# Decoded sequences' scores and values: heads modulo four in the four 32-row strips of PSUM

## The reference, cut to what matters

```python
c_all = cumsum(concat([lf_past, logf]))                    # log forget gates, per head
s_past = einsum('bqhd,bkhd->bhqk', q, k_past) * ATTN_SCALE + c_new[..., None] - c_past[:, :, None, :]
s_new = where(tri, einsum('bqhd,bkhd->bhqk', q, k) * ATTN_SCALE + c_new - c_new', -inf)
p = softmax(concat([s_past, s_new], axis=-1))
return einsum('bhqk,bkhd->bqhd', p[..., :P], v_past) + einsum('bhqk,bkhd->bqhd', p[..., P:], v)
```

## Time and profile before

| what | us |
|---|---|
| median of 3 runs | 2475.67 |
| lowest, highest | 2474.58, 2480.06 |
| the profiled execution's own time | 2478.78 |
| its span, first to last instruction | 2477.0 |
| head loop, first `page_scores` to the first L1617 | 1058.66 to 1126.62 |
| logits and softmax of the decoded sequences | 1126.62 to 1138.37 |
| values, first L1648 to the copy L1204 | 1138.37 to 1172.68 |
| `in_m` starts | 1184.66 |

### The profile page before, as it was taken

How to read it: one execution, slowest core, us unless ns; L and a number is a source line. 1 busy time by engine, 2 the same in 40 slices (tenths; PEclk the granted TensorE clock), 3 DMA queues, 4 the chain that set the end, 5 groups by cost and what they waited for, 6 DMA issues and landing times.

```text
span 2477.0 us, 47822 instructions
## 1 busy us (share of the span) xinstructions
PE 2400.4 (97%) x17547; PEld 2329.1 (94%) x17547; DVE 1248.7 (50%) x1850; ACT 843.6 (34%) x1109; POOL 83.7 (3%) x96
## 2 busy tenths in 40 slices
PE   7999999999999999898899897999999999999998
PEld 6999999999999999687899775999999999999998
DVE  6554444444554554552457675465444444455443
ACT  4333333333333443320234323343333333333322
POOL 2000000000000000000000241000000000000000
PEclk9999999999999999898999887999999999999999
DMA  6555555555544455433355341455555445555553
GB/s 165 170 166 169 163 163 170 171 165 169 165 163 164 151 165 165 137 123 134 122 162 162 117 118 38 163 160 166 166 169 161 162 170 170 169 162 160 170 161 131
DMA packets 175655, 383.82 MB, mean 155 GB/s; under 512 B 18949, under 2 KB 44669, under 8 KB 175245
## 3 DMA queue, kind: packets, MB, share of 16 engines
q1 hardware_dynamic: 172736, 375.98, 47.9%
q0 software_dynamic: 2432, 5.57, 0.7%
q10 hardware_dynamic: 416, 1.32, 0.2%
HBM read 373.09 MB, written 9.70 MB: 155 GB/s over the span
## 4 chain that ended last, share of the span: by engine, by line
PE 93%; DVE 4%; ACT 1%; issue 1%; DMA 0%; POOL 0%; ACTq 0%; DVEq 0%; POOLq 0%
PE ps L1415 28%; PE ps L1417 28%; PE ps L1416 28%; PE ps L1597 1%; PE ps L1654 1%; DVE w_lo L846 1%; PE ps L1760 1%; PE ps L1584 1%; PE ps L1461 1%; PE ps L1751 1%; PE ps L1498 1%; PE ps L1468 1%; PE ps L1532 0%; PE ps L1555 0%; DVE xt L872 0%
## 5 line engine op out<-in xcount | busy, mean ns | idle before, releaser
L846 DVE TENSOR_TENSOR w_lo<-w_raw,w_hi 128x1024 fp32r<-128x1024 f32 (+1 forms) x690 | 788.9, 1185 | 1038.3 <-ACT w_hi L560 1037.7
L560 ACT CAST w_hi<-w_raw 128x1024 fp32r<-128x1024 f32 (+1 forms) x690 | 669.3, 1018 | 1304.2 <-PE ps L1417 1301.2
L1415 PE MATMUL ps<-x_hi,w_hi 128*128 128x288 f32 (+1 forms) x2752 | 815.8, 296 | 5.2 <-DVE w_lo L846 3.2
L1417 PE MATMUL ps<-x_hi,w_lo 128*128 128x288 f32 (+1 forms) x2752 | 813.3, 296 | 0.0
L1416 PE MATMUL ps<-x_lo,w_hi 128*128 128x288 f32 (+1 forms) x2752 | 807.9, 294 | 0.0
L1415 PEld LDWEIGHTS ps<-x_hi,w_hi 128*128 128x128 f32 x2752 | 517.0, 188 | 6.4 <-DVE w_lo L846 3.3
L1416 PEld LDWEIGHTS ps<-x_lo,w_hi 128*128 128x128 f32 x2752 | 521.4, 189 | 0.1
L1417 PEld LDWEIGHTS ps<-x_hi,w_lo 128*128 128x128 f32 x2752 | 517.8, 188 | 0.0
L1415 PE MATMUL ps<-hid_hi,w_hi 128*128 (+1 forms) x1376 | 407.2, 296 | 1.5 <-DVE X L1017 1.5
L1416 PE MATMUL ps<-hid_lo,w_hi 128*128 (+1 forms) x1376 | 406.9, 296 | 0.0
L1417 PE MATMUL ps<-hid_hi,w_lo 128*128 (+1 forms) x1376 | 406.8, 296 | 0.0
(11 more groups left out here) (408 smaller groups left out, 1573.2 us busy)
## 6 DMA issues: line engine op xcount, KB each, us to landing
w_raw<-in_w_down SPq DMA_DIRECT2D x178, 512.0 KB
w_raw<-in_w_gate SPq DMA_DIRECT2D x320, 256.0 KB
w_raw<-in_w_up SPq DMA_DIRECT2D x320, 256.0 KB
w_raw<-in_w_in SPq DMA_DIRECT2D x64, 512.0 KB
w_raw<-in_w_in SPq DMA_DIRECT2D x64, 384.0 KB
w_raw<-in_w_out SPq DMA_DIRECT2D x32, 512.0 KB
page<-in_cache_k SPq DMA_DIRECT2D x16, 512.0 KB, 3.5
w_raw<-in_w_gate SPq DMA_DIRECT2D x32, 192.0 KB
```

The source lines that it names most:

```text
L560: nc.scalar.copy(w_hi[:, slot, 0:width], w_raw[:, slot, 0:width]).then_inc(w_hi_ready, 1)
L846: nc.vector.tensor_tensor(w_lo[:, slot, 0:width], w_raw[:, slot, 0:width], w_hi[:, slot, 0:width].bitcast(F32), ALU.subtract).then_inc(w_l ...
L1415: mm(out, hi, x_hi[:, k, :], start=first and pair == 0 and s == slots[0], stop=False)
L1417: ins = mm(out, lo, x_hi[:, k, :], start=False, stop=last and pair == 1 and s == slots[-1])
```

## The change

Heads are put in strips by h % 4, and the rows are ordered (h, b, q) in place of (b, h, q).

- `page_scores`: head h of a page writes strip h % 4 of bank 6; heads h and h + 4 share a strip and lie 256 columns apart, and the page half c takes 128 columns. `qz` for sequence b now has, per head, all 32 (b, q) query columns with all but sequence b's zeroed; sequences add up in place.
- New tokens: the products swap their operands (queries stationary, keys moving) and write in four strips of bank 5, at once where the logits are built. The copy `STn`, its semaphore and the two products L1633 go.
- `nl_new`, `nl_past`, `spread`, `PTn` follow the new order; `spread` shrinks to 32x128, the copy to `PTn` becomes plain.
- Values: head h writes strip h % 4 of bank 2 (columns by h // 4), for new tokens and pages. The result is 128x256, so that one copy and two transposes of 128x128 stand in place of two copies and eight transposes.

The diff:

```diff
--- before.py
+++ after.py
@@ -128,7 +128,7 @@
     mask_t = t_("mask_t", [P, 3 * P])
     mask4_q = t_("mask4_q", [SM, SM])
     mask4_t = t_("mask4_t", [SM, SM])
-    spread = t_("spread", [SM, NB * SM])
+    spread = t_("spread", [SM, P])
     sel = t_("sel", [H, H, P], F32R)
     one_hot = t_("one_hot", [P, H, H])
     vecs = t_("vecs", [P, 146])
@@ -217,7 +217,7 @@
             qz = nl_past
 
 
-            pz, out_rows = kpT[:, 0, :].rearrange("p (r n) -> p r n", r=4), kpT[0:SM, 1, :]
+            pz, out_rows = kpT[:, 0, :].rearrange("p (r n) -> p r n", r=4), kpT[:, 1, 0:2 * HD]
 
             flat = [x[:, :, :].rearrange("p h t -> p (h t)") for x in (qa, ka)]
             v_page = ([kn[:, i, :] for i in range(3)] + [page[:, (NB * NPG + i) % 3, :] for i in range(3)]
@@ -225,8 +225,7 @@
             VRING = len(v_page)
 
 
-            PTs, STn = l_("PTs", [P, 512]), l_("STn", [SM, 256])
-            PTn = STn
+            PTs, PTn = l_("PTs", [P, 512]), l_("PTn", [SM, 256])
             Ps = l_("Ps", [P, 2, T])
 
         scope, l_ = area("left")
@@ -749,8 +748,7 @@
                                      accum_out=den[:, k, g2:g2 + 1]).then_inc(sem("sample_exp"), 1)
         act.wait_ge(sem("sample_pT"), 1)
         nc.scalar.copy(PTs[:, :], ps[:, 0, :]).then_inc(sem("sample_pT_ready"), 1)
-        nc.scalar.copy(PTn[:, :].rearrange("p (h b q) -> p b h q", h=H, b=NB),
-                       ps[0:SM, 1, 0:256].rearrange("p (b h q) -> p b h q", b=NB, h=H)).then_inc(sem("sample_pT_ready"), 1)
+        nc.scalar.copy(PTn[:, :], ps[0:SM, 1, 0:256]).then_inc(sem("sample_pT_ready"), 1)
 
 
 
@@ -1031,9 +1029,8 @@
         nc.vector.tensor_scalar(neg_upper4[:, :], upper4[:, :], -1.0, None, ALU.mult)
         nc.vector.tensor_scalar(mask4_q[:, :], lower4[:, :], -1.0, BIG, ALU.add, ALU.mult)
         nc.vector.tensor_scalar(mask4_t[:, :], upper4[:, :], -1.0, BIG, ALU.add, ALU.mult)
-        nc.vector.tensor_copy(spread[:, :].rearrange("p (b h q) -> p b h q", b=NB, h=H),
-                              ident[0:SM, 0:SM].rearrange("p (b q) -> p b q", q=TS).unsqueeze(2)
-                              .to_broadcast([SM, NB, H, TS]))
+        nc.vector.tensor_copy(spread[:, :].rearrange("p (j s) -> p j s", j=4),
+                              ident[0:SM, 0:SM].unsqueeze(1).to_broadcast([SM, 4, SM]))
         nc.vector.memset(one_hot[:, :, :], 0.0).then_inc(sem("one_hot_zero"), 1)
         dve.wait_ge(sem("one_hot_zero"), 1)
         for h in range(H):
@@ -1146,9 +1143,9 @@
             if b >= 2:
                 dve.wait_ge(sem("sT_done"), NPG * (b - 1))
             nc.vector.tensor_tensor(
-                qz[:, b % 2, :].rearrange("p (h g q) -> p h g q", h=H, g=H),
-                qa[:, :, TP + b * TS:TP + (b + 1) * TS].unsqueeze(1).to_broadcast([P, H, H, TS]),
-                one_hot[:, :, :].unsqueeze(3).to_broadcast([P, H, H, TS]), ALU.mult).then_inc(sem("qz_ready"), 1)
+                qz[:, b % 2, :].rearrange("p (h g q) -> p h g q", h=H, g=NB),
+                qa[:, :, TP:T].rearrange("p h (g q) -> p h g q", g=NB),
+                one_hot[:, b, :].unsqueeze(1).unsqueeze(3).to_broadcast([P, H, NB, TS]), ALU.mult).then_inc(sem("qz_ready"), 1)
 
         dve.wait_ge(sem("qk_normed"), 2 * H)
         queries_apart(0)
@@ -1165,18 +1162,16 @@
                 o_copy(h - 1)
         o_copy(H - 1)
 
-        nc.vector.tensor_scalar(nl_new[:, :].rearrange("p (b h q) -> p b h q", b=NB, h=H),
-                                LF[0:SM, 2, 0:H].unsqueeze(1).unsqueeze(3).to_broadcast([SM, NB, H, TS]), -1.0, None, ALU.mult)
+        nc.vector.tensor_scalar(nl_new[:, :].rearrange("p (h s) -> p h s", h=H),
+                                LF[0:SM, 2, 0:H].unsqueeze(2).to_broadcast([SM, H, SM]), -1.0, None, ALU.mult)
         dve.wait_ge(sem("lf_past_loaded"), 16 * NB * NPG)
         dve.wait_ge(sem("sT_done"), NB * NPG)
         for c in range(NPG):
             last = nc.vector.tensor_scalar(
-                nl_past[:, c, :].rearrange("p (b h q) -> p b h q", b=NB, h=H),
-                lf_past[:, :, :].rearrange("p (b c) h -> p b c h", c=NPG)[:, :, c, :].unsqueeze(3)
-                .to_broadcast([P, NB, H, TS]), -1.0, None, ALU.mult)
+                nl_past[:, c, :].rearrange("p (h b q) -> p h b q", b=NB, h=H),
+                lf_past[:, :, :].rearrange("p (b c) h -> p h b c", c=NPG)[:, :, :, c].unsqueeze(3)
+                .to_broadcast([P, H, NB, TS]), -1.0, None, ALU.mult)
         last.then_inc(sem("nl_ready"), 1)
-        dve.wait_ge(sem("sT_done"), NB * NPG + 1)
-        nc.vector.tensor_copy(STn[:, :], ps[0:SM, 7, 0:256]).then_inc(sem("sT_ready"), 1)
         dve.wait_ge(sem("sample_logits"), 1)
         nc.vector.tensor_reduce(mx[:, 0, :], ps[:, 6, :].rearrange("p (g s) -> p g s", g=2), AX.X, ALU.max)
         link(nc.vector.tensor_reduce(mx[:, 1, :], ps[:, 5, 0:2 * SM].rearrange("p (g s) -> p g s", g=2), AX.X, ALU.max))
@@ -1196,12 +1191,10 @@
                 dve.wait_ge(sem("sample_pv"), p - 3)
             nc.vector.tensor_tensor(
                 pz[:, p % 4, :].rearrange("p (h b q) -> p h b q", h=H, b=NB),
-                PTs[:, c * 256 + b * SM:c * 256 + (b + 1) * SM].rearrange("p (h q) -> p h q", h=H).unsqueeze(2)
-                .to_broadcast([P, H, NB, TS]),
+                PTs[:, c * 256:(c + 1) * 256].rearrange("p (h b q) -> p h b q", h=H, b=NB),
                 one_hot[:, b, :].unsqueeze(1).unsqueeze(3).to_broadcast([P, H, NB, TS]), ALU.mult).then_inc(sem("pz_ready"), 1)
         dve.wait_ge(sem("sample_pv"), NB * NPG)
-        for half in range(2):
-            nc.vector.tensor_copy(out_rows[:, half * 512:(half + 1) * 512], ps[0:SM, 2 + half, :]).then_inc(sem("out_rows_ready"), 1)
+        nc.vector.tensor_copy(out_rows, ps[:, 2, 0:2 * HD]).then_inc(sem("out_rows_ready"), 1)
         dve.wait_ge(sem("sample_oT"), 1)
         nc.vector.tensor_copy(ya[:, :, TP:T], ps[:, 1, 0:256].rearrange("p (h s) -> p h s", h=H)).then_inc(
             sem("ya_ready"), 1)
@@ -1592,10 +1585,10 @@
             pe.wait_ge(sem("kpT_hi"), p + 1)
             pe.wait_ge(sem("qz_ready"), b + 1)
 
-            r, col = b % 4 * SM, b // 4 * 256 + c * P
             for h in range(H):
+                r, col = h % 4 * SM, h // 4 * 256 + c * P
                 ins = mm(ps[r:r + SM, 6, col:col + P], qz[:, b % 2, h * SM:(h + 1) * SM],
-                         kpT[:, p % 2, h * HD:(h + 1) * HD], start=b < 4 and c == 0 and h == 0,
+                         kpT[:, p % 2, h * HD:(h + 1) * HD], start=p == 0 and h < 4,
                          stop=True, skip_group_check=True)
             ins.then_inc(sem("sT_done"), 1)
 
@@ -1612,9 +1605,10 @@
                 values(h - 1)
             page_scores(2 * h + 1)
         values(H - 1)
-        bhq = lambda x: x.rearrange("p (b h q) -> p b h q", b=NB, h=H)
         for h in range(H):
-            ins = mm(bhq(ps[0:SM, 7, 0:256])[:, :, h, :], ka[:, h, TP:T], qa[:, h, TP:T], start=True, stop=True)
+            r = h % 4 * SM
+            ins = mm(ps[r:r + SM, 5, h // 4 * SM:(h // 4 + 1) * SM], qa[:, h, TP:T], ka[:, h, TP:T], start=h < 4,
+                     stop=True, skip_group_check=True)
         ins.then_inc(sem("sT_done"), 1)
 
 
@@ -1626,15 +1620,13 @@
             mm(o0, nl_past[:, 0, r], upper[:, :], **add)
             mm(o1, nl_past[:, 0, r], ones[:, :], **add)
             mm(o1, nl_past[:, 1, r], upper[:, :], **add)
-        pe.wait_ge(sem("sT_ready"), 1)
         for g2 in range(2):
             r = slice(g2 * P, (g2 + 1) * P)
             o2 = ps[:, 5, g2 * SM:(g2 + 1) * SM]
-            mm(o2, STn[:, r], ident[0:SM, 0:SM], start=True, stop=True)
             mm(o2, nl_past[:, 0, r], ones[:, 0:SM], **add)
             mm(o2, nl_past[:, 1, r], ones[:, 0:SM], **add)
             mm(o2, nl_new[:, r], upper4[:, :], **add)
-            ins = mm(o2, spread[:, r], mask4_q[:, :], **add)
+            ins = mm(o2, spread[:, :], mask4_q[:, :], **add)
         ins.then_inc(sem("sample_logits"), 1)
         for g2 in range(2):
             pe.wait_ge(sem("sample_p"), g2 + 1)
@@ -1645,18 +1637,20 @@
         pe.wait_ge(sem("sample_pT_ready"), 2)
 
         for h in range(H):
-            mm(ps[0:SM, 2 + h // 4, h % 4 * HD:(h % 4 + 1) * HD], PTn[:, h * SM:(h + 1) * SM],
-               vn[0:SM, 2, h * HD:(h + 1) * HD], start=h % 4 == 0, stop=True, skip_group_check=True)
+            r = h % 4 * SM
+            mm(ps[r:r + SM, 2, h // 4 * HD:(h // 4 + 1) * HD], PTn[:, h * SM:(h + 1) * SM],
+               vn[0:SM, 2, h * HD:(h + 1) * HD], start=h < 4, stop=True, skip_group_check=True)
         for p in range(NB * NPG):
             pe.wait_ge(sem(f"v_loaded{p % VRING}"), 16 * (p // VRING + 1))
             pe.wait_ge(sem("pz_ready"), p + 1)
             for h in range(H):
-                ins = mm(ps[0:SM, 2 + h // 4, h % 4 * HD:(h % 4 + 1) * HD], pz[:, p % 4, h * SM:(h + 1) * SM],
+                r = h % 4 * SM
```

(7 more changed lines are left out.)

## The result

The changed kernel takes 2438.2 us (median of 4 runs, 2432.9 to 2440.3), the kernel before beside it 2477.5; the ratio is 0.9839, with a 95% interval of 0.9828 to 0.9851. That is 39.9 us less on the base of the forecast, which said 30.2 less. The direction and the place were right, the size was not. On the forecast's base the ratio gives 2435.8 us, where the forecast said 2445.5 and its rival B 2435.

What follows compares the result with a forecast made beforehand. PE was taken to bound the kernel; scores 14.0, logits 0.8, values 14.7 and output rows 0.7 sum to 30.2 us saved, 2475.67 to 2445.5 us, with a range of 2438 to 2475.

Steps and rivals of the forecast that it cites:

- rival B: Scores and values: records overlap regardless of pairs, down to 0.033 us each, saving 20 and 19.3 us; 2435; chance 0.10.
- What bounds the kernel: Whole kernel: PE, busy 2400.4 of 2477.0 us, so what its attention-stage lines give up is kernel time.
- The scores' term, 14.0: Head loop, `page_scores`: one streaming time a head, 0.88 us a page in place of 1.75, saving 14.0 us.
- Copies to `kpT`: Head loop: DVE's copy, 0.88 us earlier, would start at 1071.31, still after its mask work ended at 1070.70.
- Logits 0.8 and output rows 0.7: Behind the loop, dropping the L1633 pairs saves 0.76 us; after the values, one copy and fewer transposes save 0.7.
- The values' term, 14.7: Values stage: one streaming time a head, 0.875 us a page at full clock, 19.6 us in place of 34.3.
- neither binds: Values stage: loads of pages 10 to 15 land in time; page 10 needed at about 14 us, page 15 at 18.4.
- one of my own signs of a wrong prediction: Attention stage: its ending with PE waiting for `kpT` copies or pages would show the prediction wrong.
- Rivals A: Scores and values: PE streams one moving operand at a time whatever the strip; only 1.5 us saved, 2474.2; chance 0.18.
- D: Scores and values: PE empties and reloads at each strip change, 0.11 to 0.20 us each; 2503 to 2527; chance 0.06.
- The range: Whole kernel: 2438 to 2475 us, taking in the forecast with its clock bounds, partial overlap and strips changing nothing.

## Why the prediction was right or wrong

**What bounds the kernel: right.** The time came out of PE's streams in the attention stage, and nothing of it was lost on the way to `in_m`: 41.3 us by stages, 40.5 at its start after a loop that began 0.8 later.

**The scores' term, 14.0: wrong, 20.4 measured.** The step that failed is "If PE starts records in order, the chain is one streaming time for each head, not two and not a quarter". It is a quarter. A strip's second record waits in that strip, and the records of other strips go past it. The saving was 1.28 us a page (1.86 to 0.58) instead of 0.875. For the first page, at 1.2 GHz, it was 2.44 instead of 1.71, of which the work behind it at that clock gave about half back: up to the second page's products 1.25 us were left (5.70, from 1058.66 to 1064.36, became 4.45, from 1059.49 to 1063.94), where I had 0.9. I had priced this case as the prediction's rival B and put 0.10 on it, on the argument that two records share a strip; nothing in the trace of before spoke for or against the order among strips. That rival was right in its sum (20 and 19.3 us) and wrong in its floor: 0.033 us a record was an upper bound taken from 32-column products, and the strip's own streaming, 4 x 0.109 = 0.44, decides before it.

**Copies to `kpT`: right.** With a page shortened by 1.28 instead of 0.88 DVE still finished its mask work in time: it waits for PE 0.19 us ahead of the second copy. With ACT at 2.49 and DVE at 4.40 of 6.07 us the engines behind PE still fit.

**Logits 0.8 and output rows 0.7: right,** 0.75 and 0.85.

**The values' term, 14.7: wrong, 19.35 measured,** by the same step, and here with a new bound: pages 10 to 15, of which I had said that "neither binds", because I let page 10 be needed 14 us after the start. It was needed at 8.2 (1126.26, without a marked wait), and pages 11 to 15 waited. A stage that ends with PE waiting for pages was one of my own signs of a wrong prediction, and it came. Under rival B I had worked out 15.0 us for the stage, and 14.96 were measured, but this agreement is in part luck: B had loads of 1.66 us each, which lets page 11 land 7.6 us after the start and page 15 at 14.2. PE began page 11 at 9.2 and page 15 at 14.25, so the loads came 1.27 us apart, but later. The two errors cancel. The clock also rose sooner than the forecast had it, about 6.7 us after the start instead of 8.9.

**Rivals A (strips change nothing) and D (a price for each change of strip): refuted.** A change of strip costs nothing that the trace shows: at full clock a page of 16 records in four strips takes four streaming times. The Trainium skill, "TensorE: Matmul & The Clock Gate", Part 3, has products in strict order of start and end and loads that overlap only with another row group; the traces differ from both. With eight records of a strip in a row, a record of one strip (`page`, 1123.55) starts behind one of the next strip (`kn`, 1123.35) that stands after it in the program; and the loads lie beside the streams though every product uses the same 128 rows (16 loads in 0.38 us at 1067.18). The speedup of 2.38 that the same section gives for three column tiles is repeated by no run here; four gave 1.86 / 0.58 = 3.2 for a page.

**The range** (2438 to 2475) left rival B out with 0.10 on it, and by the ratio the result, 2435.8 on the base of the forecast, lies below it.

## What to carry to other kernels

Small fp32 products whose stationary operand has 32 columns ran four at a time here once neighbours in the program wrote different 32-row strips of PSUM: count the records of the fullest strip (two for each fp32 product), and keep no more than four of one strip in a row. When such a stream gets three to four times faster, look at once for what feeds it: here it was the ring of value pages, and with three more places for pages the stage was 3.6 us shorter and the median 5.5 us lower. In four of nine traces with waits or pauses in the values the granted clock fell right behind them, so the last waits of a stage may cost more than they show.

## What the runs showed of the hardware

- Four strips stream side by side at both clock levels: 0.58 us for a page of 16 fp32 records at 2.4 GHz, 1.01 at 1.2 GHz; two strips 1.00, one strip 1.86.
- With eight records of a strip in a row, the last four of a strip ran beside the first four of the next, twelve times one and one in the second pair of pages. A pair took 20 streaming times at first and 17 later, where eight is full overlap; with four in a row a page took 0.60 us instead of 0.58. It fits a strip that holds four records, which no record shows by itself.
- Behind the same values stage, with PE waiting for loads at its end, the granted clock was 0.62 in one execution and 1.00 in another, 1.5 us apart at the next step.
